# Moving the page products of decode attention from GpSimd to VectorE, and folding two small instructions

## The reference, cut to what matters

```python
def diff_attention(q, q_pos, k, v, k_pos, lam):
    ...
        s = jnp.einsum('bqhcd,bkhcd->bhcqk', qi, k).astype(jnp.float32) * scale
        s = jnp.where(mask, s, -jnp.inf)
        p = jax.nn.softmax(s, axis=-1)
        a = p[:, :, 0] - lam * p[:, :, 1]
        return jnp.einsum('bhqk,bkhe->bqhe', a.astype(v.dtype), v)
```

## Time and profile before

| | us |
|---|---|
| time of three runs: median (lowest to highest) | 2285.85 (2284.49 to 2289.54) |
| span of the profiled execution, first to last instruction | 2291.0 |
| busy: TensorE, VectorE, ScalarE, GpSimd | 2122.5, 1003.8, 664.0, 630.0 |

### The profile page before, as it was taken

The page is one execution under the profiler, slowest core; times in us unless marked ns, Lnnn a source line. Parts: engine busy times, 40 slices in busy tenths (PEclk is TensorE's granted clock), DMA queues, the critical chain, the costliest instruction groups (busy, mean ns, idle before and its releaser), DMA issues.

```text
span 2291.0 us, 40108 instructions
## 1 busy us (share of the span) xinstructions
PE 2122.5 (93%) x16466; PEld 2032.9 (89%) x16466; DVE 1003.8 (44%) x1125; ACT 664.0 (29%) x961; POOL 630.0 (27%) x394
## 2 busy tenths in 40 slices
PE   7999999866489999999999999999866999999997
PEld 7999999755379999999999999999744599999997
DVE  4333333899944333333433333333499333333222
ACT  4222222444343222222113222222233232222221
POOL 1333200555613333301312333201343023333211
PEclk9999999988779999999999999999977999999998
DMA  5333332211012333332342333333353322333430
GB/s 162 92 92 91 104 89 83 64 40 44 28 31 83 92 92 92 112 89 74 107 124 85 91 91 92 111 89 114 103 165 101 110 65 85 90 91 92 113 89 37
DMA packets 347165, 206.26 MB, mean 90 GB/s; under 512 B 6115, under 2 KB 338276, under 8 KB 346940
## 3 DMA queue, kind: packets, MB, share of 16 engines
q1 hardware_dynamic: 339044, 191.31, 28.4%
q10 hardware_dynamic: 6856, 7.53, 1.0%
q0 software_dynamic: 1184, 6.28, 0.8%
HBM read 198.52 MB, written 7.53 MB: 90 GB/s over the span
## 4 chain that ended last, share of the span: by engine, by line
PE 81%; DVE 13%; issue 3%; ACT 1%; POOL 1%; DVEq 0%; DMA 0%; POOLq 0%; ACTq 0%; SPq 0%
PE ps_all L499 76%; DVE conv_b L1139 2%; DVE conv L1139 2%; DVE pr L1267 2%; PE ps_all L675 1%; DVE w_lo L1038 1%; DVE mx L1258 1%; DVE s_dec L1333 1%; PE ps_all L562 1%; PE ps_all L508 1%; DVE at_n L1270 1%; PE ps_all L572 1%; PE ps_all L637 0%; PE ps_all L596 0%; POOL inv L1479 0%
## 5 line engine op out<-in xcount | busy, mean ns | idle before, releaser
L499 PE MATMUL ps_all<-xg_hi,w_hi 128*128 128x260 f32 x3456 | 710.8, 287 | 66.9 <-DVE w_lo L1038 54.9
L795 ACT ACTIVATE w_hi<-raw 128x1024 fp32r<-128x1024 f32 (+1 forms) x296 | 334.5, 1130 | 1296.5 <-PE ps_all L499 1295.1
L499 PE MATMUL ps_all<-xg_hi,w_lo 128*128 128x260 f32 x3456 | 702.8, 285 | 0.0
L499 PE MATMUL ps_all<-xg_lo,w_hi 128*128 128x260 f32 x3456 | 702.6, 285 | 0.0
L499 PEld LDWEIGHTS ps_all<-xg_hi,w_hi 128*128 128x128 f32 x3456 | 542.1, 191 | 70.7 <-DVE w_lo L1038 67.3
L499 PEld LDWEIGHTS ps_all<-xg_lo,w_hi 128*128 128x128 f32 x3456 | 539.7, 191 | 0.0
L499 PEld LDWEIGHTS ps_all<-xg_hi,w_lo 128*128 128x128 f32 x3456 | 539.5, 191 | 0.0
L1038 DVE TENSOR_TENSOR w_lo<-raw,w_hi 128x1024 fp32r<-128x1024 f32 (+1 forms) x296 | 402.1, 1358 | 268.4 <-ACT w_hi L795 268.4
L499 PE MATMUL ps_all<-h_hi,w_hi 128*128 128x260 f32 x1664 | 341.4, 285 | 5.2 <-DVE h_lo L1207 5.2
L499 PE MATMUL ps_all<-h_hi,w_lo 128*128 128x260 f32 x1664 | 338.9, 283 | 0.0
L499 PE MATMUL ps_all<-h_lo,w_hi 128*128 128x260 f32 x1664 | 338.4, 283 | 0.0
(11 more groups left out here) (162 smaller groups left out, 1327.7 us busy)
## 6 DMA issues: line engine op xcount, KB each, us to landing
raw<-w_in SPq DMA_DIRECT2D x176, 512.0 KB, 3.7
raw<-w_out SPq DMA_DIRECT2D x64, 704.0 KB, 4.5
raw<-c_in SPq DMA_DIRECT2D x16, 512.0 KB, 3.8
raw<-w_kv SPq DMA_DIRECT2D x16, 512.0 KB, 3.8
page<-cache_k SPq DMA_DIRECT2D x16, 512.0 KB, 4.6
page<-cache_v SPq DMA_DIRECT2D x14, 512.0 KB, 4.3
raw<-c_out SPq DMA_DIRECT2D x8, 512.0 KB, 3.8
raw<-w_q SPq DMA_DIRECT2D x8, 512.0 KB, 3.8
```

The lines of the kernel that those rows point to most:

```text
L499: mm = nc.tensor.matmul(unit[slot][:, s, :], w[:, c % 2, k * P:(k + 1) * P], m[:, s * HALF:(s + 1) * HALF], start=kk == 0 and i == 0, stop ...
L795: nc.scalar.activation(w_hi[:, c % 2, 0:w], raw[:, c, 0:w], ACT.Copy).then_inc(hi_made, 1)
```

## The change

VectorE now makes the page product itself, directly ahead of its reduction, and waits for page and `qb`; GpSimd keeps the powers and one memset. The factor SCALE is multiplied into q where it leaves PSUM (phase "q"), so that the exponentials need no scale and the maximum can be written negated by the reduction itself (L1259 goes). Minus lambda becomes the second scalar of the scaling (L1266 goes). The maximum of the sample scores is treated likewise.

```diff
@@ activations in attention
-                                                 scale=SCALE, bias=nmx[:, s % 2, c:c + 1],
+                                                 bias=nmx[:, s % 2, c:c + 1],
@@ rotary, phase "q"
-                        scaled(t_gate[:, r % 2, :], c % 2).then_inc(drained, 1)
+                        if ph.kind == "q":
+                            nc.vector.scalar_tensor_tensor(halves(t_gate[:, r % 2, :]), unit[c % 2], SCALE, halves(rstd[:, :]),
+                                                           ALU.mult, ALU.mult).then_inc(drained, 1)
+                        else:
+                            scaled(t_gate[:, r % 2, :], c % 2).then_inc(drained, 1)
@@ maxima
-                    link(nc.vector.tensor_reduce(mx[:, s % 2, :], ps_all[:, 2 * (s % 2):2 * (s % 2) + 2, 0:keys], AX.X, ALU.max))
-                    nc.vector.tensor_scalar(nmx[:, s % 2, :], mx[:, s % 2, :], -SCALE, None, ALU.mult).then_inc(max_done, 1)
+                    nc.vector.tensor_reduce(nmx[:, s % 2, :], ps_all[:, 2 * (s % 2):2 * (s % 2) + 2, 0:keys], AX.X, ALU.max,
+                                            negate=True).then_inc(max_done, 1)
@@ combine
-                    link(nc.vector.tensor_tensor(rl2[:, e:e + 1], rl[:, e, 1:2], neglam[:, :], ALU.mult))
-                    link(nc.vector.tensor_scalar(pr[:, e, 1, 0:keys], pr[:, e, 1, 0:keys], rl2[:, e:e + 1], None, ALU.mult))
+                    link(nc.vector.tensor_scalar(pr[:, e, 1, 0:keys], pr[:, e, 1, 0:keys], rl[:, e, 1:2], neglam[:, :],
+                                                 ALU.mult, ALU.mult))
@@ VectorE, steps 4 to 19
-                        b, g = divmod(s - 4, NPG)
-                        dve.wait_ge(kprod_done, s - 3)
+                        i = s - 4
+                        b, g = divmod(i, NPG)
+                        dve.wait_ge(k_page_full[i % len(K_SLOTS)], 16 * (i // len(K_SLOTS) + 1))
+                        if g == 0:
+                            dve.wait_ge(qb_full[b % 2], 16 * (b // 2 + 1))
+                        nc.vector.tensor_tensor(kprod[:, :], K_SLOTS[i % len(K_SLOTS)], qb[:, b % 2, :], ALU.mult
+                                                ).then_inc(kprod_done, 1)
+                        dve.wait_ge(kprod_done, i + 1)
@@ GpSimd
-                for i in range(NS * NPG):
...
-                    nc.gpsimd.tensor_tensor(kprod[:, :], K_SLOTS[i % len(K_SLOTS)], qb[:, b % 2, :], ALU.mult
-                                            ).then_inc(kprod_done, 1)
-                    if i % 4 == 2:
-                        head_power(i // 4)
+                for h in range(NS * NPG // 4):
+                    head_power(h)
```

More of the change, by code:

```diff
@@ L176, in trunk @@
         pages_s = place("pages_s", [1, NS * NPG], I32)
-        mx = place("mx", [P, 2, 2])
         nmx = place("nmx", [P, 2, 2])
@@ L180, in trunk @@
         rl = place("rl", [P, 2, 2])
-        rl2 = place("rl2", [P, 2])
         mx_s = place("mx_s", [P, 4])
@@ L981, in attention @@
                     if s == SCORES_AT + 1:
-                        act.wait_ge(d_max, 2)
-                        nc.scalar.activation(p_dec[:, :], ps_all[:, 7, 0:PAST + 1], ACT.Exp, scale=SCALE, bias=mx_s[:, 1:2],
+                        act.wait_ge(d_max, 1)
+                        nc.scalar.activation(p_dec[:, :], ps_all[:, 7, 0:PAST + 1], ACT.Exp, bias=mx_s[:, 1:2],
                                              accum_out=mx_s[:, 2:3]).then_inc(d_exp, 1)
@@ L1283, in sample_maxima @@
                     dve.wait_ge(d_scores, 1)
-                    nc.vector.tensor_reduce(mx_s[:, 0:1], ps_all[:, 7, 0:PAST + 1], AX.X, ALU.max).then_inc(d_max, 1)
-                    dve.wait_ge(d_max, 1)
-                    nc.vector.tensor_scalar(mx_s[:, 1:2], mx_s[:, 0:1], -SCALE, None, ALU.mult).then_inc(d_max, 1)
+                    nc.vector.tensor_reduce(mx_s[:, 1:2], ps_all[:, 7, 0:PAST + 1], AX.X, ALU.max, negate=True).then_inc(d_max, 1)
                 def sample_weights():
```

## The result

The changed kernel takes 2272.76 us (median of 6 runs, 2271.22 to 2280.19) against 2285.17 (6 runs, 2283.85 to 2289.54): a ratio of 0.9946 [0.9935, 0.9957], 12.4 us less, where 12.05 was forecast. The profiled execution after took 2273.82 us, its span 2272.0.

A forecast was written before the change was run, and what follows sets the result against it. VectorE, stalled beside GpSimd's page product, was taken to set the length of steps 4 to 19. Opening -2.7, three times four steps -7.7, rest +1.05 and -2.7 made -12.05 us: 2285.85 to about 2274 us, range 2265 to 2281.

The forecast's parts named there:

- The stall: VectorE's scaling waits while GpSimd's page product uses SBUF; removing it was to give -2.0 us in each of 15 steps.
- fourth rival: The scaling's 2 us are not GpSimd's doing and stay, with the products on top: +12.0, 2298 us; chance 0.04.
- third rival: The page product on VectorE takes 2.08 us, 0.87 more in 16 steps: 2288 us; chance 0.04.
- The folds: In 32 steps on VectorE, dropping L1266 gives net -0.13 us and dropping L1259 -0.19 us per step.
- The late power: GpSimd's power waits for VectorE's product and ends near A + 2.5 instead of A + 1.7; VectorE then waits 1.75 us.
- A: The moment when VectorE's 384-column `at_n` ends, once per head; later events are timed from it.
- second rival: GpSimd's power is not held up by VectorE's product: four steps in 19.55 us, 2271.6 us in all; chance 0.13.
- four steps: A cycle of four attention steps in steps 4 to 19, 22.64 us before, forecast at 20.07 us, or -2.57.
- the tied place: The place once per head where VectorE's 512-wide maximum needs TensorE's scores, which come after the power and L637.
- first rival: TensorE's clock stays at the upper level in the attention: four steps in 18.6 us, 2268 us in all; chance 0.14.
- the opening: Attention steps 0 to 7, to the 512-wide maximum of step 7: forecast -2.7 us, TensorE keeping some of VectorE's -5.0.
- The rest: Attention after the 512-wide maximum of step 19: +1.05 us for step 19's product, -2.7 for folds in steps 20 to 31.

The follow-up runs named there:

- folds alone: The changed kernel with the page products back on GpSimd and the small instructions still folded; 2278.85 us, 0.9959 of the kernel before.
- the split product: The changed kernel with the page product as two 512-column instructions in steps with s % 4 = 2; 2269.54 us, 0.9931 of the kernel before.

## Why the prediction was right, and where a term was off

The forecast of 2274 us is met within 1.3 us, and in the cycles by the steps that it named:

- *The stall was GpSimd's doing.* The scaling of 384 columns, the same instruction in both, took 2.62 us beside the product on GpSimd (folds alone) and 0.48 with the product on VectorE (after), while the transfers went on at a share of 0.38 (0.34 before). The one longer scaling left, 1.09 us in step 20, runs beside GpSimd's memset, as forecast. So the fourth rival, that the stall stays, falls.
- *The product costs 1.22 us on VectorE* (16 times, mean 1.216); 1.21 was taken. The slow product of the third rival, 2.08, did not occur.
- *The folds.* `var` comes 0.19 earlier, as worked out. A second scalar costs 0.06 us (0.55 against 0.49, 0.48 against 0.42 for 384 columns). The negated maximum takes 0.42 and 0.69 us for 256 and 512 columns, like the plain one.
- *The late power.* It ends at A + 2.40 (forecast 2.5) and VectorE waits 1.82 us (1.75). The second rival, a power that isn't held up, is refuted by the 1.92 us. What it would have given, four steps in 19.55 us by the forecast and about 19.3 by the estimate above, no run shows by itself: in the split product the power is 0.53 of the 0.91 us earlier (19.74), and the version that puts off the reduction (18.38) has more than the early power in it.
- *Waits for transfers* were priced at nothing: none shows among VectorE's waits after.
- *Four steps* take 20.28 us; 20.07 was forecast. Of these 0.21 us 0.15 come from the lower clock level at the tied place: the maximum came at A + 6.05, where 5.9 lay between the two levels (6.1 and 5.4). VectorE got there at A + 4.23 (4.13). The first rival, a clock that stays up, did not happen there: L635 still takes 2.08 us and the scores behind it 1.23.

**The mis-sized term is the opening.** It was put at -2.7 us and measured -4.4 on the means, and -6.2 against the first profile. VectorE's own sum up to A in step 6 was -5.0, of which 1.8 was left to TensorE, since the earlier trace rows show 2.62 us of waiting for scores in step 4. A lay 32.93, 31.00 and 29.56 us after the opening's start in the three profiles of before, and 26.02 after: on the mean -5.1. So on the mean TensorE kept nothing of VectorE's 5.0; in the opening it was at the upper level for a longer time than before. That the levels differ, and by how much the products are shorter, is shown; why the clock rises sooner isn't. After, TensorE had worked without a listed wait since 1658.90 us when the products grew shorter (from 1664.65 on); in the second profile of before it had worked so from 1654.14 to 1661.07 and stayed at the lower level. The wait that I took from one profile was the longest of the three (2.62, 1.51, and none listed in the third).

*The rest* was put at -1.65 (+1.05 and -2.7) and came out at -2.9, with a scatter of 1.8 us among profiles of one kernel. The product of step 19 cost what was forecast: from the maximum of step 19 to the next it takes 5.18 us after, 4.11 or 4.12 before, +1.07. So the folds of the later steps gave more than the 2.7 that VectorE's 71% allowed them, 3.4 us with the folds alone and 4.0 here, about the whole 3.8. The exact size isn't settled, but all five profiles of kernels with the folds have rests of 43.3 to 45.5 us and all four without them 46.6 to 50.8. The three terms over their forecast (-1.7 and -1.25) and the cycles under it (+0.4) would make -14.6; the medians show -12.4. No run here separates the remaining 2 us from the scatter outside the attention (2131.1 to 2138.1 us in profiles of one kernel). So the total was closer than its parts, and that it came within 0.4 us of the forecast gain is partly luck.

## What to carry to other kernels

Busy time of VectorE may be waiting: compare the same instruction beside a GpSimd operation and without one before calling the engine full. When work moves to VectorE, look for the small GpSimd operation on the path that now starts inside a long two-input VectorE instruction, and put a reduction there instead; here that was worth 7.7 us more without a single instruction less, about half of it in the cycles by the earlier operation and half since the reduction filled a wait. A fold inside a stall is worth nothing there until the stall goes, so parts of a change should be tried together as well as apart.

## What the runs showed of the hardware

- A GpSimd product of 2.34 us (two operands of 1024 columns) holds up a VectorE scaling that starts at nearly the same time until 0.22 us after the product's end: 2.62 us instead of 0.48 for 384 columns.
- Which VectorE instruction runs beside it decides over a small GpSimd operation. A product of two operands of 1.22 us stretches the power of four numbers per partition from 1.01 to 1.92 us, one of 0.68 us to 1.39; a reduction of 1.21 us stretches it not at all (1.01).
- GpSimd gets in between two VectorE instructions that follow each other without a gap, and the second of them is not lengthened by the power (0.68 us both). The Trainium skill, "SBUF — State Buffer", section "Who interferes with whom", calls the shared ports an exclusive lock; for VectorE as the holder these runs agree (1.92 and 1.39 us). For the power as the holder they do not show it: the second half ran its usual 0.68 us while the power was still busy, to 1697.35.
